# One block from the output projection to the combination, in a decoder layer with a mixture of experts

## The reference, cut to what matters

```python
x = x + merged @ w_out
xn = rms_norm(x, norm_ffn)
g_idx, g_w = argmax and max of softmax(xn @ w_router_group + b)       # 4 groups
top_p, top_i = top_k(softmax(the 8 fine logits of that group), 2)
gates = g_w * top_p / sum(top_p)
for e in range(32):                                                   # rows that chose e
    y_e = (silu(xb @ w_gate[e]) * (xb @ w_up[e])) @ w_down[e]
x = x + sum of gate * y over a token's two experts
y = rms_norm(x, norm_final)
```

## Time and profile before

| What | Value |
|---|---|
| Median of 3 runs (2032.97 to 2033.86) | 2033.64 us |
| The profiled execution | 2030.74 us |
| Its span in the profile | 2029.2 us |
| Share of the span: PE, PEld, DVE, ACT, POOL | 91%, 78%, 57%, 43%, 24% |
| HBM read, written | 304 MB, 46 MB |

### The profile page before, as it was taken

One profiled execution on the slowest core, in us unless ns is written; L12 is line 12 of the kernel. 1 busy time (PEld: TensorE's weight loads), 2 busy tenths in 40 slices (PEclk: granted clock), 3 DMA queues, 4 the chain that ended last, 5 costly groups with the idle time before them and its releaser, 6 DMA issues. The chain is left out here.

```text
span 2029.2 us, 29000 instructions
## 1 busy us (share of the span) xinstructions
PE 1836.7 (91%) x9856; PEld 1575.2 (78%) x9856; DVE 1156.0 (57%) x1866; ACT 874.8 (43%) x1535; POOL 493.4 (24%) x464
## 2 busy tenths in 40 slices
PE   7989997999998999999997988976999999999950
PEld 5877774999998878788885987855888888888840
DVE  4256656311111243434334444667999999999937
ACT  4245555321111222222211213345877878778724
POOL 3022323000000121203021001221675333333314
PEclk9989999999998999989997998988999999999985
DMA  7111201222213102020111453347999999999946
GB/s 190 52 48 43 53 22 42 84 67 90 63 58 106 44 25 83 21 82 24 28 58 43 139 157 117 110 174 262 391 388 384 383 386 384 385 388 390 386 172 243
DMA packets 186052, 332.99 MB, mean 164 GB/s; under 512 B 36721, under 2 KB 118033, under 8 KB 184897
## 3 DMA queue, kind: packets, MB, share of 16 engines
q1 hardware_dynamic: 163840, 277.48, 38.3%
q0 software_dynamic: 21328, 53.27, 7.4%
q10 hardware_dynamic: 816, 1.38, 0.4%
HBM read 304.04 MB, written 46.35 MB: 173 GB/s over the span
## 5 line engine op out<-in xcount | busy, mean ns | idle before, releaser
L2062 POOL DMA_INDIRECT y_d<-e_y,e_idxs x32 | 135.6, 4239 | 202.0 <-DVE e_y L2161 200.4
L2132 DVE TENSOR_TENSOR e_Lg<-e_rawg,e_Hg 128x1024 fp32r<-128x1024 f32 x128 | 148.4, 1218 | 6.7 <-ACT e_Hg L2085 6.3
L2132 DVE TENSOR_TENSOR e_Lu<-e_rawu,e_Hu 128x1024 fp32r<-128x1024 f32 x128 | 147.7, 1213 | 0.0
L2132 DVE TENSOR_TENSOR e_Ld<-e_rawd,e_Hd 128x1024 fp32r<-128x1024 f32 x124 | 143.1, 1212 | 0.0
L2085 ACT ACTIVATE e_Hg<-e_rawg 128x1024 fp32r<-128x1024 f32 x128 | 124.9, 1050 | 4.9 <-PE bank L150 4.9
L148 PE MATMUL bank<-r_wH,xH 128*128 128x512 f32 (+1 forms) x288 | 121.0, 420 | 6.3 <-DVE r_wL L1268 3.6
L2085 ACT ACTIVATE e_Hu<-e_rawu 128x1024 fp32r<-128x1024 f32 x124 | 121.0, 1059 | 0.0
L2085 ACT ACTIVATE e_Hd<-e_rawd 128x1024 fp32r<-128x1024 f32 x124 | 121.0, 1049 | 0.0
L150 PE MATMUL bank<-r_wH,xL 128*128 128x512 f32 (+1 forms) x288 | 116.1, 403 | 0.0
L149 PE MATMUL bank<-r_wL,xH 128*128 128x512 f32 (+1 forms) x288 | 115.7, 402 | 0.0
L1030 DVE TENSOR_TENSOR b_wL<-raw,b_wH 128x1024 fp32r<-128x1024 f32 x24 | 29.2, 1221 | 148.4 <-ACT b_wH L1003 148.4
(11 more groups left out here) (390 smaller groups left out, 4841.3 us busy)
## 6 DMA issues: line engine op xcount, KB each, us to landing
e_rawg<-in_w_gate SPq DMA_DIRECT2D x128, 512.0 KB, 12.2
e_rawu<-in_w_up SPq DMA_DIRECT2D x128, 512.0 KB, 10.4
e_rawd<-in_w_down SPq DMA_DIRECT2D x124, 512.0 KB, 11.9
raw<-in_w_in SPq DMA_DIRECT2D x51, 512.0 KB, 3.9
c_Y<-y_d SPq DMA_DIRECT2D x8, 1024.0 KB, 13.2
gate_t<-b_gr_s POOLq DMA_DIRECT2D x8, 528.0 KB, 3.0
m_t<-b_m_s POOLq DMA_DIRECT2D x8, 528.0 KB, 3.5
m_gate<-gate_t POOLq DMA_DIRECT2D x8, 528.0 KB, 4.1
```

What stands on the lines that cost most here:

```text
L2062: pool.indirect_dma_start(out=ch.y_d, out_offset=bass.IndirectOffsetOnAxis(ap=idx[:, e % IDX, 1:2], axis=0), in_=y[:], in_offset=None, bou ...
L2132: dve.tensor_tensor(L[kind][:, q], raw[kind][:, q], H[kind][:, q].bitcast(F32), ALU.subtract).then_inc(w_lo[kind], 1)
```

## The change

The four blocks become one: `stage_out` returns its five engine programs (`output_programs`), which run at the head of the experts' block, and beyond and combine become classes whose programs run at its end. What ordered them by a block's end is now ordered by semaphores: `served` waits for all scatters of expert results. Cut to its core:

```diff
-        with nc.Block() as block:        # stage_out, stage_beyond and stage_combine had one each
+        return Programs(sync, gpsimd, scalar, vector, tensor)
...
 # stage_out, POOL
             for t in range(NT):
-                store(t)
                 if t >= 2:
                     fill(t - 2)
+                store(t)
...
-            fill(NT - 1)
-            pool.wait_ge(ch.e_go, 1)
-            pool.wait_ge(scat, 16 * 2 * NT)
-            expert_slots(pool, ch, 0)
-            expert_gather(pool, ch, 0)
+            pool.wait_ge(ch.e_go, 1)
+            expert_gather(pool, ch, 0)           # waits e_listed
+            fill(NT - 1)
+            pool.wait_ge(scat, 16 * 2 * NT)
             expert_slots(pool, ch, 1)
             expert_slots(pool, ch, 2)
 # stage_out, ACT
             for t in range(1, NT):
                 back(t - 1)
-                front(t)
                 exponentials(t - 1)
+                act.activation(root1[:], ch.ident[0:1, 0:1], ACT.Sqrt)
+                front(t)
 # stage_out, DVE
+            def pick(t):
+                m = rows_of(t)
+                done(dve.tensor_scalar(mine[0:m], eid[0:m, t], 0.0, None, ALU.is_equal))
+                done(dve.scalar_tensor_tensor(out=key[0:m, 0:2], in0=rank[0:m, t], scalar=1.0, in1=mine[0:m], op0=ALU.add, op1=ALU.mult))
+                done(dve.scalar_tensor_tensor(out=key[0:m, 2:3], in0=key[0:m, 0:1], scalar=-1.0, in1=key[0:m, 1:2], op0=ALU.add, op1=ALU.add))
+                done(dve.tensor_tensor(entry[0:m, t, 1:2], entry[0:m, t, 1:2], mine[0:m, 1:2], ALU.add))
+                dve.tensor_scalar(sel[0:m, t], iota[0:m], key[0:m, 2:3], None, ALU.is_equal).then_inc(picked, 1)
+            def first_list():
+                dve.wait_ge(list_mm, 1)
+                done(dve.tensor_scalar(free[:], banks[4][:, 2:3], -float(NOBODY), float(NOBODY), ALU.mult, ALU.add))
+                dve.tensor_scalar(ch.e_idx[:, 0], banks[4][:, 0:2], free[:, 0:1], None, ALU.add).then_inc(ch.e_listed, 1)
...
             for t in range(1, NT):
+                if t >= 2:
+                    place(t - 2)
+                    pick(t - 2)
                 back(t - 1)
-                front(t)
                 choose(t - 1)
-                if t >= 2:
-                    place(t - 2)
+                front(t)
                 weights(t - 1)
-            back(NT - 1)
             place(NT - 2)
+            pick(NT - 2)
             split_lo("g", 0)
+            back(NT - 1)
             split_lo("g", 1)
             choose(NT - 1)
             place(NT - 1)
+            pick(NT - 1)
+            first_list()
             split_lo("g", 2)
             split_lo("g", 3)
             weights(NT - 1)
-            overflow()
+            a = overflow_counts()
+            return lambda: overflow_lists(a)
 # stage_out, PE
+            def enlist(t):
+                pe.wait_ge(picked, t + 1)
+                return pe.matmul(banks[4][:, 0:3], sel[0:m, t], entry[0:m, t, 0:3], start=(t == 0), stop=(t == NT - 1))
             for t in range(NT):
                 project(t, 0)
+                if t >= 2:
+                    count(t - 2)
                 if t >= 1:
                     turn(t - 1)
-                project(t, 1)
+                project(t, 1, 0)
                 if t >= 1:
                     route(t - 1)
-                if t >= 2:
-                    count(t - 2)
+                project(t, 1, 1)
-            turn(NT - 1)
             count(NT - 2)
+            turn(NT - 1)
             route(NT - 1)
+            for t in range(NT - 1):
+                enlist(t)
             count(NT - 1)
+            enlist(NT - 1).then_inc(list_mm, 1)
 # experts, SP, behind the loads of x2
+            sp.wait_ge(x_turned, 2 * NE)
+            sp.dma_start(rows[:], ch.norm_final.broadcast_to([P, D])).then_inc(combine.g_in, 16)
+            beyond.sync(sp)
+            combine.sync(sp)
 # experts, DVE
+            overflow_lists = output.vector(dve)
             rows_lo(0)
             split_lo("u", 0)
+            overflow_lists()
             walk(dve, body)
...
 # combine
 # SP: result tile t is stored from Y[0:m, t, 0] instead of o[0:m, t % 3]; the gain is no longer loaded here
-                    pool.tensor_tensor(x2[0:m, t], x2[0:m, t], Y[0:m, t, 0], ALU.add).then_inc(x_sum, 1)
-                    act.activation(Y[0:m, t, 0], Y[0:m, t, 0], ACT.Copy, scale=ch.gates[0:m, t, 0:1]).then_inc(y0_done, 1)
+            dve.wait_ge(self.y_in[t], 16)
+            dve.scalar_tensor_tensor(out=Y[0:m, t, 0], in0=Y[0:m, t, 0], scalar=self.ch.gates[0:m, t, 0:1], in1=x2[0:m, t],
+                                     op0=ALU.mult, op1=ALU.add).then_inc(self.half, 1)
+            dve.wait_ge(self.half, t + 1)
             dve.scalar_tensor_tensor(out=Y[0:m, t, 1], in0=Y[0:m, t, 1], scalar=self.ch.gates[0:m, t, 1:2], in1=Y[0:m, t, 0], ...)
-                    if t >= OB:
-                        dve.wait_ge(o_st[s], 16 * (t // OB))
-                    dve.scalar_tensor_tensor(out=o[0:m, s], in0=Y[0:m, t, 1], ...)
+            dve.scalar_tensor_tensor(out=Y[0:m, t, 0], in0=Y[0:m, t, 1], ...)
```

More of the change, by code:

```diff
@@ L11 @@
 import math
+from collections import namedtuple
 from contextlib import ExitStack
@@ new lines, in sync @@
+        def sync(sp):
+            for t in range(NT):
+                m, s = rows_of(t), t % 2
+                if t >= 2:
+                    sp.wait_ge(add_done, t - 1)
+                src = ch.x_sample if t == NB else ch.x_prompt[t * P:(t + 1) * P, :]
+                sp.dma_start(xin[0:m, s], src).then_inc(x_in[s], 16)
+                if t == 1:
+                    sp.wait_ge(lo_done, KT)
+                    for dst, src in ((iota, ch.c["iota"]), (entry, ch.c["entries"]), (groups, ch.c["groups"]), (before, ch.c["before"]), (ones, ch.c["ones"])):
+                        sp.dma_start(dst[:], src).then_inc(table_in, 16)
+                    sp.dma_start(ch.tokens[:], ch.c["tokens"]).then_inc(table_in, 16)
+            sp.wait_ge(mm_done, NT)
+            for kind in "gud":
+                for q in range(NQ):
+                    expert_chunk(sp, ch, kind, 0, q)
@@ new lines, in scalar, with front, back, exponentials @@
+        def scalar(act):
+            for q in range(KT):
+                act.wait_ge(w_in[q], 16)
+                act.activation(wH[:, :, q * P:(q + 1) * P], raw(q), ACT.Copy).then_inc(hi_done, 1)
+            def front(t):
+                m, s = rows_of(t), t % 2
+                act.wait_ge(add_done, t + 1)
+                act.activation(junk[0:m], x2[0:m, s], ACT.Square, accum_out=stat[0:m, s, 0:1]).then_inc(sq_done, 1)
+                act.wait_ge(ms_done, t + 1)
+                act.activation(stat[0:m, s, 2:3], stat[0:m, s, 1:2], ACT.Sqrt).then_inc(root_done, 1)
+            def back(t):
+                m = rows_of(t)
+                act.wait_ge(turned, t * 2 + 1)
+                act.wait_ge(r_mm, t)
+                act.activation(xT[:, 0:4, 0:m], banks[4][:].rearrange("p (k i) -> p k i", k=4)[:, :, 0:m], ACT.Copy).then_inc(t_out0, 1)
+            def exponentials(t):
+                m = rows_of(t)
+                act.wait_ge(keyed, t + 1)
+                act.activation(eg[0:m], lg[0:m, 0:NG], ACT.Exp, bias=less[0:m, 0:1], accum_out=den[0:m, 0:1]).then_inc(e_done, 1)
+                act.activation(den[0:m, 1:2], fm8[0:m, 1:2], ACT.Exp, bias=less[0:m, 1:2]).then_inc(e_done, 1)
+            def split_hi(kind, qs):
+                for q in qs:
+                    act.wait_ge(ch.e_w_in[kind][q], 16)
+                    act.activation(ch.e_H[kind][:, q], ch.e_raw[kind][:, q], ACT.Copy).then_inc(ch.e_w_hi[kind], 1)
+            front(0)
+            for t in range(1, NT):
+                back(t - 1)
+                exponentials(t - 1)
+                act.activation(root1[:], ch.ident[0:1, 0:1], ACT.Sqrt)
+                front(t)
+            split_hi("g", (0, 1))
+            back(NT - 1)
+            split_hi("g", (2, 3))
+            exponentials(NT - 1)
+            split_hi("u", range(NQ))
@@ L1992, in stage_experts @@
+def stage_experts(nc, ch, output, x2_at):
     sem = ch.sem
@@ L2120, in body @@
                         out_evac(e - 1)
+                output.scalar(act)
                 rows_hi(0)
@@ L2238, in _ @@
                     pe.sem_inc(used[kind], NQ)
+                output.tensor(pe)
                 turn_rows(0)
```

861 lines of the change are left out of this document (409 added, 452 removed).

## The result

The changed kernel takes 2012.99 us in the median of four runs (2010.31 to 2014.95) against 2033.31 us before (four runs, 2032.26 to 2033.86): a ratio of **0.9899, 95% interval 0.9886 to 0.9912**. The forecast was 2011.6 us. The profiled execution took 2014.95 us, with a span of 2013.4.

A forecast was written before the change was run, and what follows sets the result against it. PE was taken to bound the output projection and experts' loop, leaving the gaps between stages to move; -2.6 + 0.8 - 11.7 - 8.5 = -22.0 gave a median of 2011.6 us, range 2003.5 to 2020.5.

The forecast's parts named there:

- The block's end: Last scatter to first combination load: SP waits for landings itself, POOL's 9.04 us DRAIN runs beside the combination; -11.7 us.
- The combination: After the experts: two DVE sums replace POOL's addition and the slow sum, tile period 5.10 to 4.32; -8.5 us.
- the three buffers' wait: In the combination: storing results from already consumed rows removes a buffer wait never seen, so no gain was counted.
- Rival F: In the combination: 3.36 us is the sum's own price, not POOL's doing; +16 there, total about +3, 2037; chance 0.02.
- The loop of the output projection: Early routing turns it from PE-bound to bound through DVE and ACT, period 14.24 to 14.9; last scaled row +6.7 us.
- The walk: Output projection: steps timed from X, one normalized row's end, to the next at X + 14.9, then on to expert 0's gather.
- Rival A: Output projection loop stays PE-bound: last scaled row only +2.2, sum -26.5, 2007 us; chance 0.2.
- Rival E: Output projection: pauses lower PE's clock, some 11 us more per affected tile; with three tiles 2045; chance 0.05.
- Rival C: Output projection: an ACT table switch costs a second 1.28 us, +10 over eight tiles, 2022 us; chance 0.04.
- The list and expert 0: Behind the last scaled row: list summed on chip, gather issued after 12.35 against 20.3 us, landing in 6.1.
- Rival B: Expert 0 starts late: its gather lands in 11.2 us among the weights, 5 us more, 2016.5; chance 0.18.
- The overflow lists: Start of the experts' loop: the overflow count's second half, 4.3 us of DVE, comes through to PE as +0.8 us.

The follow-up runs named there:

- own_block: Changed kernel with the combination put back in a block of its own; 2022.67 us, ratio 0.9941.
- pool_busy: Changed kernel with POOL given an unused 128x1024 addition per tile beside DVE's sums in the combination; 2033.36 us, ratio 1.0003.
- stage_bufs: Changed kernel with the combination's results written to three buffers of their own instead of over the loaded rows; one execution, 2017.33 us.
- root_again: Changed kernel with ACT's exponentials of the tile before moved behind the square and root; second series, 2004.93 us, ratio 0.9859.
- no_preload: Changed kernel without the dummy square root that loads ACT's table ahead of the square; 2014.68 us, ratio 0.99.
- list_hbm: Changed kernel with expert 0's list written to memory and read back instead of summed on chip; 2016.32 us, ratio 0.991.

## Why the prediction was right

**The block's end, -11.7 forecast, -11.8 measured.** own_block gives +11.6 for its return. The drain's cover was there as said.

**The combination, -8.5 forecast, -8.95 measured.** Period 4.33 against 4.32, first landing 4.98 against 5.1; pool_busy confirms the reason. One step failed, and luck kept it out of the sum: "the three buffers' wait, which was not seen, goes for nothing". stage_bufs shows that the faster combination would have met that wait, 2.4 us: the first store then lands in 13.9 where the longest took 9.5 before, and its buffer is wanted after 13.0. The sum was right only because the change also took the wait away. Rival F is out, but its price was added up wrongly. By the earlier trace rows two sums at 3.36 would have added some 4.2 us a tile to the 4.32, 38 in nine tiles; the combination would have cost about 29 more than before and not 16, and the total would have come out some 16 slower, not 3.

**The loop of the output projection, +6.7 forecast, +6.2 measured.** The walk holds step by step: router's product at X + 3.76 (3.65), `front` at X + 8.70 (8.6), next X at + 14.8 (14.9), PE waiting 0.40 to 0.44 a tile and 0.73 in the first (0.65). Rival A (PE stays the limit) is out for this kernel, though 0.5 us in 14.8 decide it; root_again, at 5.0 less, is what A (4.5 less) would have been. Rival E did not happen: with a pause in every tile the clock stayed at 1.00. Rival C's second table cost did not either: the dummy root starts 1.30 behind the load's start, and the period came out under the forecast. By the 2.66 us a switch of the Trainium skill, "ScalarE: Activation LUTs", section What ACT_TABLE_LOAD costs, the loop would have been some 11 us longer as an estimate; the trace of both kernels, and no_preload's, disagrees. One reading was off: the prediction has the square root's result 1.5 us ahead of the row's scaling, but in the kernel before the load starts 1.73 ahead of it and the root itself 0.44:

```profile
1295.07 0.20 ACT L1715 ACTIVATE o_stat<-o_stat 128x1 f32<-128x1 f32 x1
```

What the argument needs, that the root follows 1.29 behind the load's start, stands.

**The list and expert 0, -9.3 forecast behind X8, -8.6 measured.** The term that was mis-sized is the gather's issue: X8 + 12.35 in the walk, 13.21 measured. I had 0.1 to 0.4 for the list's product; what came was 3.58 us of list products at the lower clock, queued ahead of the last count, and a wait of 1.42 for DVE. I had costed the last product alone and not asked which stood in front of the count. The landing, 6.1 forecast, was 6.06, for a better reason than "between the two", if the windows are read rightly: it ends when the prefetched weights are through. Rival B's 11.2 was met in none of the twelve profiles after the change; the longest was 7.39.

**The overflow lists, +0.8 forecast, +1.4 measured**, and 0.5 to 2.1 over the profiles in which this part is the same. No run isolates it.

**What the sum hid.** The terms were off by -0.5 (loop), +0.85 (issue), +0.6 (experts) and -0.45 (combination), and much of that cancels, so a sum within 0.4 of the 21.65 is in part luck. Nor does a right sum say that each part pays. Alone, the block is worth 11.6, the results over loaded rows 2.4, the list on chip 4.4 to 4.7 (list_hbm), and the early routing, as ordered on ACT, is a loss of 2.6 in the stretches that it touches.

## What to carry to other kernels

When a stage is moved ahead in a loop that one engine bounds, look at what each other engine now has queued between the step that came earlier and the step that the bound waits for: here small exponentials ahead of a table load cost 5 of 6 us, and moving one line gave them back. A wait that is absent from a trace may appear once its neighbours get faster, so a buffer is judged at the new period, with the longest landing and not the median one, and that landing can itself grow when its store goes out earlier among the loads (9.5 to 13.9 us here). And once a request goes out earlier, see what is already in the transfer queues: the last 0.9 us that the list gained was lost in the landing, by the windows to weights prefetched ahead of it.

## What was not expected of the hardware

The first result store took 13.9 us to land in stage_bufs (the longest took 13.3 in the changed kernel and 9.5 before) where the median store takes 2.6; it was issued while nine loads of 1 MB or less were under way. And DVE's sum beside POOL's addition ends 1.07 to 1.08 us behind the end of POOL's instruction in two kernels with additions of 2.60 and 2.34: it looks held, not slowed, although in one of them its own row starts first.
